# Semaphores cleared at the opening of the next stage, in a kernel of two transformer blocks

## The reference

```python
h = h + mixed(chunked_attention(q, k, v, rel_bias), s5_mixer(u, ...)) @ w_out
h = h + memory_attention(rmsnorm(h), rmsnorm(mem), ...)
h = h + peer_ffn(rmsnorm(h), w_q, sub_keys, u_tab, v_tab)      # experts: 128 x 128 rows of u and v
# second block, on the output of the first
x = x + g1 * ((gates[0] * dilated_attention(...) + gates[1] * differential_attention(...)) @ w_out)
x = x + g2 * peer_ffn(rmsnorm(x) * (1 + sc2) + sh2, w_query, sub_keys, expert_u, expert_v)
```

## Time and profile before

| what | value |
|---|---|
| median of the runs shown | 3743.4 us (3 runs, 3740.94 to 3743.43) |
| time of the profiled execution | 3741.82 us |
| its span, first to last instruction | 3740.0 us |
| PE busy | 3586.7 us, 96% |
| DVE, ACT, POOL busy | 2966.7, 1713.2, 676.8 us |
| granted clock of PE, mean share of full | 0.984 |

### The profile page before, as it was taken

The page is one execution under the profiler, slowest core; times in us unless marked ns, Lnnn a source line. Parts: engine busy times, 40 slices in busy tenths (PEclk is TensorE's granted clock), DMA queues, the critical chain, the costliest instruction groups (busy, mean ns, idle before and its releaser), DMA issues. The chain is left out here.

```text
span 3740.0 us, 54632 instructions
## 1 busy us (share of the span) xinstructions
PE 3586.7 (96%) x19470; PEld 3146.0 (84%) x19470; DVE 2966.7 (79%) x6558; ACT 1713.2 (46%) x3277; POOL 676.8 (18%) x523
## 2 busy tenths in 40 slices
PE   8868999999999999999899989999999999999999
PEld 7546778999999988888788757789999999888887
DVE  4674653898988899999777495547998888899998
ACT  4424443333666633333444464343335666433333
POOL 0000000000322244444100000000003222344442
PEclk9989999999999999999999999999999999999999
DMA  4352323455899899999522103324558999899997
GB/s 150 129 183 85 108 68 102 138 168 177 308 314 305 296 375 403 400 401 398 206 86 92 47 1 107 99 71 136 165 169 284 312 308 314 325 402 400 400 401 293
DMA packets 371886, 853.47 MB, mean 228 GB/s; under 512 B 35728, under 2 KB 184848, under 8 KB 368912
## 3 DMA queue, kind: packets, MB, share of 16 engines
q1 hardware_dynamic: 258912, 530.84, 40.5%
q0 software_dynamic: 73728, 268.47, 19.3%
q10 hardware_dynamic: 38976, 50.68, 3.8%
HBM read 753.26 MB, written 95.42 MB: 227 GB/s over the span
## 5 line engine op out<-in xcount | busy, mean ns | idle before, releaser
L1321 POOL DMA_INDIRECT p2f_row<-in_expert_u_rows,p2f_index x128 | 167.3, 1307 | 1302.0 <-POOLq L83 1007.7
L1321 POOL DMA_INDIRECT p1f_row<-in_peer_u_rows,p1f_index x128 | 169.6, 1325 | 973.8 <-POOLq L83 680.2
L1979 PE MATMUL p1v_out<-p1a_u_hi,p1v_w_hi 128*128 128x512 f32 x768 | 299.2, 390 | 0.0
L1979 PE MATMUL p1v_out<-p1a_u_lo,p1v_w_hi 128*128 128x512 f32 x768 | 298.9, 389 | 0.0
L1979 PE MATMUL p2v_out<-p2a_u_hi,p2v_w_hi 128*128 128x512 f32 x768 | 298.8, 389 | 0.0
L1979 PE MATMUL p2v_out<-p2a_u_hi,p2v_w_lo 128*128 128x512 f32 x768 | 298.8, 389 | 0.0
L1979 PE MATMUL p1v_out<-p1a_u_hi,p1v_w_lo 128*128 128x512 f32 x768 | 298.8, 389 | 0.0
L1979 PE MATMUL p2v_out<-p2a_u_lo,p2v_w_hi 128*128 128x512 f32 x768 | 298.8, 389 | 0.0
L1485 ACT CAST p2a_u_hi<-p2a_u 128x1024 fp32r<-128x1024 f32 x128 | 135.1, 1055 | 281.5 <-PE p2v_out L1979 281.5
L1485 ACT CAST p1a_u_hi<-p1a_u 128x1024 fp32r<-128x1024 f32 x128 | 135.1, 1056 | 277.5 <-PE p1v_out L1979 277.5
L1321 POOL DMA_INDIRECT p2f_row<-in_expert_v,p2f_index x128 | 167.9, 1312 | 257.7 <-DVE p2f_sum L1344 228.8
(11 more groups left out here) (731 smaller groups left out, 10792.8 us busy)
## 6 DMA issues: line engine op xcount, KB each, us to landing
p1a_u<-in_peer_u SPq DMA_DIRECT2D x128, 512.0 KB, 4.1
p1a_u<-in_peer_v SPq DMA_DIRECT2D x128, 512.0 KB, 8.3
p2a_u<-in_expert_u SPq DMA_DIRECT2D x128, 512.0 KB, 4.2
p2a_u<-in_expert_v SPq DMA_DIRECT2D x128, 512.0 KB, 8.1
gates<-p_kept SPq DMA_DIRECT2D x20, 2048.0 KB, 15.3
acts<-p1a_a ACTq DMA_DIRECT2D x128, 192.0 KB, 3.8
p1w_a<-acts SPq DMA_DIRECT2D x128, 192.0 KB, 7.1
acts<-p2a_a ACTq DMA_DIRECT2D x128, 192.0 KB, 3.9
```

What stands on the lines that cost most here:

```text
L1321: self.nc.gpsimd.indirect_dma_start(self.row[:, n % self.RING, :], None, self.u_rows if dot else self.v_rows, bass.IndirectOffsetOnAxis(ap ...
L1979: last = nc.tensor.matmul(out[:, o, :], lhs[:, s, t * P:(t + 1) * P], rhs[:, n % VSLABS, cols], start=(n == 0 and m == 0), stop=(n == KEYS ...
```

## The change

`clear` is gone. When a stage's tools end, its semaphores go on a list, `RETIRED`. The function `open_block` opens every stage in place of `nc.Block()`: it first clears and frees what is on the list, and no meeting follows. At the end of the program one clear and one meeting remain. The cut shows the first of 14 equal edits of a block's opening; they stand for the 27 stages.

```diff
+RETIRED = []
+
+
+def open_block(nc, ctx):
+
+    if RETIRED:
+        nc.clear_and_free_semaphores(list(RETIRED))
+        RETIRED.clear()
+    return ctx.enter_context(nc.Block())
+
+
 def phase_tools(nc, ctx, tag):
...
     taken = []
 
-    def clear():
-
-        nc.clear_and_free_semaphores(taken)
-        nc.all_engine_barrier()
-
     def sem(name):
         if not taken:
-            ctx.callback(clear)
+            ctx.callback(lambda: RETIRED.extend(taken))
         taken.append(nc.alloc_semaphore(f"{tag}_{name}"))
         return taken[-1]
...
-        block = ctx.enter_context(nc.Block())
+        block = open_block(nc, ctx)
...
     A["out"] = nc.dram_tensor("out_0", (SEQ, D), F32, kind="ExternalOutput").ap()
+    RETIRED.clear()
     program(nc, A)
+    nc.clear_and_free_semaphores(list(RETIRED))
+    nc.all_engine_barrier()
+    RETIRED.clear()
```

More of the change, by code:

```diff
@@ L2539, in opening @@
         zeroed, cols_in = sem("zeroed"), sem("cols_in")
-        block = c.enter_context(nc.Block())
+        block = open_block(nc, c)
         @block.gpsimd
```

## The result

| | before | after |
|---|---|---|
| median of 5 runs each on one chip | 3740.94 us | 3721.84 us |
| lowest and highest | 3738.24, 3743.43 | 3719.95, 3725.24 |
| profiled execution, time and span | 3741.8, 3740.0 us | 3719.95, 3718.2 us |
| granted clock of PE, mean share of full | 0.984 | 0.987 |

A forecast was written before the change was run, and what follows sets the result against it. PE, 96% busy, or a chain feeding it sets the pace inside stages; the closings between them lie wholly on the path. 20.7 - 1.35 - 0.4 - 0.1 = 18.9 us (18.85) off gives 3724.5 us, range 3716 to 3732.

The forecast's parts named there:

- The closings: Second meetings and clears between the block's release and the last release, at 27 places: 20.7 us off the path.
- the end: End of the program: one meeting and seven clears stay on the path, 0.30 + 7 x 0.15 = 1.35 us.
- the first place: First boundary: ACT waits for the load of x anyway, so nothing is gained there; -0.4 us.
- the mask: Chunk attention: POOL's memset, behind two clears, could come a little late for DVE's first use; -0.1 us.
- The gathers: Four stages: POOL starts 0.3 to 0.75 us late; PE's products don't need them; nothing taken, at most 2.4 us.
- the larger number of clears: 87 clears on POOL between stages in place of 46: cost nothing elsewhere, as POOL is busy for 18%.
- no net effect: PE's clock behind the openings: some low stretches, up to 1.7 us each, come or go; no net change, range widened.
- a sign of being wrong: Ten-us clock windows behind the 26 openings: the prediction would be wrong if they differed by more than three openings.
- shorter idle, better clock: Rival at the openings: 0.6 us less idle spares four of 14 the lower clock, 6.8 us more, 3718; chance 0.16.
- The fetching of instructions: Rival at the boundaries: the closing hid instruction fetches, so all the gain could go, 3743 us; chance 0.05.
- Something late on POOL: Rival: gathers behind the clears (2.4 us) and two more openings at the lower clock (3.4), 3730 us; chance 0.08.
- The changed phase: Rival: the 12 openings with full clock fall to the lower level, costing 41 us, 3765; chance 0.03.

The follow-up runs named there:

- Four_meetings: Changed kernel with four bare meetings of all engines ahead of the clears at each of the 26 later openings; ratio to before 1.0055, median 3762.70 us.
- clear_then_meet: Changed kernel with one meeting of all engines put back behind the clears at each of the 26 later openings; ratio to before 1.0014, median 3743.38 us.
- meet_then_clear: Changed kernel with one meeting of all engines put back ahead of the clears at each of the 26 later openings; ratio to before 0.9971, median 3729.87 us.
- the shifted starts: Changed kernel with three or six bare meetings at the first opening alone, starting 1 or 2 us later; ratios to before 0.9945 and 0.9948.
- before_again: The kernel before, unedited, in another group of runs for a second trace; median 3742.45 us.
- after_again: The changed kernel, unedited, in another group of runs for a second trace; ratio to before 0.9953, median 3721.76 us.

## Why the prediction was right

**The mechanism.** The closings lay on the path in full. Their 20.7 us, read from before, came out to the tenth in a second trace of it, and after has none between stages. The start of `p1g` moved from 921.4 to 912.6, 8.8 us where some 9 were forecast. That it fits so closely is luck: the second pair of traces has 923.7 and 911.0, 12.7 us, as the stages ahead of it scatter.

**The terms.** Predicted net 18.9; the closings' part measured in the trace is 17.7 + 1.3 = 19.0, and the time fell by 19.1 by the medians and 20.2 by the ratio. The sum is that close because small errors cancel: the end was 0.35 us too cheap, and the 0.5 us taken off for the first place and the mask belong to the stages, not to the closings.
- The end was undersized: 1.70 us where I had 1.35. A meeting is 0.336 and not 0.30, and the seven clears with their drains took 0.19 each, as two of the ranges are wide (134 and 157 ns).
- The first place can't be told. ACT started at 5.18 where it had started at 5.69, as the load of x landed earlier in this trace, and the first norm scatters between 14.3 and 16.3 us over all 14 traces. The 0.4 us neither stands nor falls.
- The memset of the mask cost 0.06 us against the first trace of before and 0.37 against the second; I had 0.1. That POOL is now the releaser was forecast as possible and is so.
- The gathers were rightly priced near nothing but for a wrong reason. I wrote that by the code PE's products of `p1g` don't need the gather. They do, with 5.45 us of DVE and ACT between. At 0.3 to 0.65 us of delay the product is 0.2 us later; at 2.2 us it is 2.0. The bound of 2.4 us that I kept for the range was of the right kind.
- That the larger number of clears costs nothing elsewhere holds for after as far as its traces tell, but for the 0.1 to 0.2 us of `gb`. With three times the clears 12 of the 27 stages kept the length of after to 0.1 us in both traces, and the others differ mostly by the clock.

**The clock.** I took no net effect. The time fell by 0.1 us (medians) or 1.2 us (ratio) more than the closings' 19.0; that is what is left for the clock and for everything else. After has 14 of 26 windows below 1.00, as before, for instance:

```profile
363.60:373.60 10.00, 9.89 (x47) 8.86 (x48) 6.96 (x12) 8.36 (x17) 0.00 (x0) 0.83 0.35 111
...
1829.60:1839.60 10.00, 5.25 (x30) 5.25 (x31) 2.90 (x8) 7.00 (x12) 0.00 (x0) 0.66 0.30 105
```

`wmq` had 1.00 before and has 0.83 now. The number agrees by luck: three openings lost the full clock and three others gained it, six in all, where I had named more than three as a sign of being wrong. That sign was badly chosen, as the same kernel's two traces differ in one opening (before) and in three (after). The sum of what is missing to 1.00 fell from 3.05 to 2.84. Over the whole run the lower level lasted 118.6 and 119.3 us in the two traces of before, 100.2 and 99.7 in those of after. Over 18 runs of before, 0.001 of mean clock went with 1.2 us, and over 15 others with 1.7; from 0.985 to 0.987 that is an estimated 2.4 to 3.4 us. The stages gave 2.8 and 1.6 us, but the first norm, which has none of the lower level, is 1.4 us shorter in the first pair and 1.6 longer in the second. Without it they gave 1.3 and 3.2 us. The rival "shorter idle, better clock" had the sign right, but it counted on four spared openings and 6.8 us. Four_meetings with its 160.7 us speaks for the idle time as the cause. Against it stands that the nine traces without meetings at the later openings range from 88.6 to 112.3 us, and clear_then_meet and meet_then_clear have 110.5 and 107.5. So it is not shown.

**The rivals that fell.** The fetching of instructions exists at one opening of 26, `gb`, and costs 0.1 to 0.2 us there, not the 19 of the rival; it was not there before, so a closing did not hide it either. At the others the 0.1 us of before is 0.1 us after. Something late on POOL exists, but at a tenth of the size. The changed phase put no row of openings at the lower level.

## What to carry to other kernels

A meeting at a boundary cost its length each time here, though PE is busy for 96% of the span, and a clear between two meetings cost all five engines what it cost one. Put such housekeeping behind the release, on the engine that does it, and read the first work of that engine in every stage: where a memset or a gather stands there, let the housekeeping wait for the next boundary. A dependency that the code seems not to have is best read from a fixed distance between two starts over several traces. And before a difference between two traces is explained, take a second trace of each kernel: here it undid two neat readings, of the start of `p1g` and of the shifted starts.

## What the runs showed of the hardware beyond that

- Some stages repeat very closely: 47.06, 15.72 and 255.1 us, to 0.1 us over 13 of the 14 traces; four_meetings, with more of the lower level, has 49.60 and 17.42 in the first two and the same 255.1. The first norm, with none of the lower level, scatters by 2 us all the same.
- The lower level comes back in many of the same stages. Its time agrees to 0.2 us in 21 of 27 stages between before and before_again, and in 17 between after and after_again. The stage behind the chunk attention has 18 to 28 us of it in every kernel, while the two long stages of 255 us have none in any.
- A range clear of 71 semaphores takes 416 ns and one of 86 takes 500; the clears of before take 44 to 218.
